# Sample rows of the mixer's output normed, turned and routed one block earlier, in both layers of a decoder step

## What is computed

```python
xp = layer_norm(ALPHA * xp + hp, ln_mix_g[i], ln_mix_b[i])      # 256 prompt rows
xs = layer_norm(ALPHA * xs + hs, ln_mix_g[i], ln_mix_b[i])      # 64 sample rows
aff = sigmoid(x @ router)                  # 32 affinities per token
grp = argmax over 4 groups of the sum of the two best (aff + bias)
eidx = the two best experts in that group; wts = aff[eidx] / sum
out = sum over the two experts of wts * (silu(x @ w_gate[e]) * (x @ w_up[e])) @ w_down[e]
x = layer_norm(ALPHA * x + out, ln_ffn_g[i], ln_ffn_b[i])
```

## Time and profile before

| | us |
|---|---|
| median of 3 runs | 1170.09 |
| lowest, highest | 1162.45, 1173.85 |
| profiled execution, its time | 1163.89 |
| span of that execution (first to last instruction) | 1160.5 |
| mean granted TensorE clock | 0.970 |
| busy: PE / DVE / ACT / POOL | 1063.1 / 455.1 / 234.7 / 131.2 |

### The profile page before, as it was taken

One profiled execution on the slowest core, in us unless ns is written; L12 is line 12 of the kernel. 1 busy time (PEld: TensorE's weight loads), 2 busy tenths in 40 slices (PEclk: granted clock), 3 DMA queues, 4 the chain that ended last, 5 costly groups with the idle time before them and its releaser, 6 DMA issues. The chain is left out here.

```text
span 1160.5 us, 13972 instructions
## 1 busy us (share of the span) xinstructions
PE 1063.1 (92%) x4918; PEld 544.3 (47%) x4918; DVE 455.1 (39%) x1167; ACT 234.7 (20%) x552; POOL 131.2 (11%) x197
## 2 busy tenths in 40 slices
PE   8899999998999989998888799899899899998883
PEld 6577767674334543333333466455554433333321
DVE  0788655546655552211111833222114522211117
ACT  0211223115001311111111313322113121111112
POOL 0000104100000011111110022320000111111010
PEclk9899999999999999999998799999999999999997
DMA  7129511205354989999998765563258599999993
GB/s 283 66 107 363 210 73 45 108 30 223 145 225 156 414 348 425 425 420 425 423 422 352 278 221 174 171 220 125 110 235 336 176 419 425 420 424 421 421 370 117
DMA packets 54913, 312.01 MB, mean 269 GB/s; under 512 B 13058, under 2 KB 13954, under 8 KB 34242
## 3 DMA queue, kind: packets, MB, share of 16 engines
q1 hardware_dynamic: 43426, 298.04, 64.3%
q0 software_dynamic: 11264, 12.61, 3.3%
q10 hardware_dynamic: 160, 0.52, 0.1%
HBM read 300.61 MB, written 33.59 MB: 288 GB/s over the span
## 5 line engine op out<-in xcount | busy, mean ns | idle before, releaser
L1402 PE MATMUL ps<-ring,xsT 128*64 128x512 f32 x704 | 160.9, 610 | 22.1 <-DMA ring<-in_experts 17.8
L1757 DVE TENSOR_TENSOR work<-work,ps 128x256 f32<-128x256 f32 x32 | 13.5, 421 | 268.6 <-ACT work L1486 268.6
L434 PE MATMUL ps<-XT,ring 128*128 128x320 f32 x384 | 108.1, 446 | 9.8 <-DMA ring<-in_w_in 5.3
L1402 PEld LDWEIGHTS ps<-ring,xsT 128*64 128x64 f32 x704 | 54.6, 140 | 125.4 <-issue 117.7
L434 PEld LDWEIGHTS ps<-XT,ring 128*128 128x128 f32 x384 | 75.3, 197 | 41.8 <-issue 7.5
L1402 PE MATMUL ps<-hi,xsT 128*64 128x512 f32 x320 | 75.7, 628 | 8.6 <-DMA hi<-in_experts 8.6
L1429 PE MATMUL ps<-ring,hT 128*64 128x512 f32 x352 | 80.4, 598 | 1.5 <-ACT hT L1490 0.9
L366 PE MATMUL ps<-XT,ring 128*128 128x320 f32 x256 | 76.9, 445 | 0.0
L1551 POOL DMA_INDIRECT y_dram<-ys,index x32 | 32.4, 1012 | 376.3 <-DVE ys L1789 333.7
L1327 PE MATMUL ps<-C 128*128 128x512 f32 x140 | 71.6, 631 | 0.6 <-PEq L836 0.3
L1543 POOL DMA_INDIRECT XT<-x_dram,index x32 | 32.8, 1024 | 314.0 <-DVE index L1686 282.3
(11 more groups left out here) (358 smaller groups left out, 1390.4 us busy)
## 6 DMA issues: line engine op xcount, KB each, us to landing
ring<-in_experts SPq DMA_DIRECT2D x36, 2048.0 KB, 24.5
ring<-in_experts SPq DMA_DIRECT2D x60, 1024.0 KB, 22.2
hi<-in_experts SPq DMA_DIRECT2D x20, 2048.0 KB, 24.6
hi<-in_experts SPq DMA_DIRECT2D x20, 1024.0 KB, 27.5
ring<-in_w_in SPq DMA_DIRECT2D x9, 2048.0 KB, 12.4
ring<-in_latent SPq DMA_DIRECT2D x60, 256.0 KB, 4.3
ring<-in_w_out SPq DMA_DIRECT2D x4, 2048.0 KB, 7.4
ring<-in_state SPq DMA_DIRECT2D x4, 1024.0 KB, 7.8
```

The lines of the kernel that those rows point to most:

```text
L434: return pe.matmul(ps[:, q, 0:TOK], ring[:, u, k * 512 + q * P:k * 512 + (q + 1) * P], XT[:, k, :], start=(k == 0), stop=(k == KD - 1))
L1402: mm = pe.matmul(ps[e * SLOTS:(e + 1) * SLOTS, GU[p], :].rearrange("p (g f) -> p g f", g=2), xsT[:, p, k, e * SLOTS:(e + 1) * SLOTS], w[:, ...
```

## The change

The class `PromptNorm` becomes `RowNorm`: every operation takes `ROWS[t]` rows, and the sample tile t = 2 goes through it at the end of the block ahead. `add_rows(v, 2)` waits for `split_done`. TensorE does three fill matmuls, then the sample tile's transposes and router matmuls (`sample_logits`); its PSUM banks are `2 * (t % 2)` and the next. ScalarE does `sample_rows`, the sigmoid's table load among it. The store of the sample rows moves from ScalarE's queue to SyncE's, behind the loads of the block's last expert. The expert block loses these operations, and six calls of idle work with them; its ScalarE begins with the sigmoids. The memset of `aff` covers 64 rows of one tile instead of all.

In the window, `turn_weights` moves behind `gate_up(0)`, ScalarE's copy of them behind `rows_in(0)`, VectorE's `weigh` behind `rows_in(0)`, and the idle call ahead of `gate_up(1)` is left out. The sample tile no longer counts in `order`, the index by which later norm steps wait.

In the diff, `expert_layer`'s lists stand behind those of the block ahead (shown for layer 0; `attend` has the same lines, the store behind `first_expert(sp, 1, 2)`).

```diff
+        FILL = 3
-        class PromptNorm:
+        class RowNorm:
...
             def turn_rows(self, pe, t):
+                r, bank = ROWS[t], 2 * (t % 2)
                 pe.wait_ge(self.norm_set, t + 1)
                 for half in range(2):
                     for k in range(4):
                         at = (4 * half + k) * P
-                        tr = pe.transpose(ps[:, 2 * t + half, k * P:(k + 1) * P], X[:, t, at:at + P], ident)
+                        tr = pe.transpose(ps[:, bank + half, k * P:k * P + r], X[0:r, t, at:at + P], ident[0:r, 0:r])
                     tr.then_inc(self.x_turned, 1)
+
+            def sample_logits(self, pe):
+                for _ in range(FILL):
+                    pe.matmul(ps[:, self.GB, :], ident, C[:, 0:512], start=True, stop=True)
+                self.turn_rows(pe, 2)
+                self.logits(pe, 2)
...
             def add_rows(self, v, t):
...
-                v.wait_ge(self.rows_done, t + 1)
+                if t == 2:
+                    v.wait_ge(self.split_done, 1)
+                else:
+                    v.wait_ge(self.rows_done, t + 1)
...
+            def sample_rows(self, act):
+                self.statistics(act, 2)
+                act.activation(self.junk[:, 0:1], eps[:, 0:1], ACT.Sigmoid)
+                self.flipped_act(act, 2)
...
                      sp.wait_ge(wout_used, 4)
                     first_expert(sp, 0, 3)
+                    norm.store(sp, 2)
...
 +                    norm.sample_logits(pe)
...
 +                    norm.sample_rows(act)
...
 +                    norm.add_rows(v, 2)
+                    norm.scale_rows(v, 2)
+                    norm.flipped_dve(v, 2)
...
 -                    idle_work(5, 6)
-                    turn_rows(pe, 0, 2)
-                    idle_work(1, 6)
-                    pe.wait_ge(xt_act, 1)
-                    pe.wait_ge(xt_dve, 1)
-                    router_logits(pe, 2).then_inc(logit_done, 1)
-
                     idle_work(8, 6)
...
                         idle_work(4, 6)
-                        turn_weights()
                         turn(w, 0)
                         gate_up(0)
+                        turn_weights()
                         turn(w, 1)
                         for j in range(PAIRS):
                             if j + 1 < LAST:
-                                idle_work(1, MAP)
+                                if j:
+                                    idle_work(1, MAP)
                                 gate_up(j + 1)
...
 -                    statistics(act, 0, 2, 0)
-                    act.activation(spare[:, 0:1], eps[:, 0:1], ACT.Sigmoid)
-                    act.wait_ge(norm_set, 1)
-                    act.dma_start(x_dram[SAMPLE, :], X[0:ROWS[2], 2, :]).then_inc(x_out, 16)
-                    flipped_act(act, 0, 2)
-                    act.wait_ge(logit_done, 1)
...
+                        rows_in(0)
                         act.wait_ge(comb_turned, 1)
                         act.activation(comb[:, :], ps[:, MAP, 0:TOK], ACT.Copy).then_inc(comb_in, 1)
-                        rows_in(0)
...
 ...
-                    step.mark(v.memset(aff[:, :, :], 0.5))
+                    step.mark(v.memset(aff[64:P, 2, :], 0.5))
...
+                        rows_in(0)
                         weigh(each)
-                        rows_in(0)
```

More of the change, by code:

```diff
@@ L259, in norm_columns, with __init__ @@
             return tr
-        class PromptNorm:
+        class RowNorm:
             GB = 6
-            def __init__(self, s, layer, junk):
+            def __init__(self, s, layer, junk, split_done=None):
                 (self.rows_done, self.summed, self.mean_set, self.squared, self.std_set, self.inverted, self.norm_set,
@@ L270, in __init__ @@
                      "n_gb_made", "n_gb_set", "n_x_turned", "n_xt_act", "n_xt_dve"])
-                self.layer, self.junk = layer, junk
+                self.layer, self.junk, self.split_done = layer, junk, split_done
             def turn_columns(self, pe):
@@ L312, in flipped_dve @@
                 for k in range(4, KD):
-                    ins = v.tensor_scalar(XT[:, k, OFF[t]:OFF[t] + P], ps[:, 2 * t + 1, (k - 4) * P:(k - 3) * P],
+                    ins = v.tensor_scalar(XT[:, k, OFF[t]:OFF[t] + ROWS[t]],
+                                          ps[:, 2 * (t % 2) + 1, (k - 4) * P:(k - 4) * P + ROWS[t]],
                                           gb[:, 0, 0, k:k + 1], gb[:, 0, 1, k:k + 1], ALU.mult, ALU.add)
@@ L839, in states_and_output @@
                 Cm = buf(st, "Cm", [P, GROUPS, 2, 4 * 40])
-                norm = PromptNorm(s, 0, Cm[:, :, :, :].rearrange("p g u x -> p (g u x)")[:, 0:D])
+                norm = RowNorm(s, 0, Cm[:, :, :, :].rearrange("p g u x -> p (g u x)")[:, 0:D])
                 pmask = buf(st, "pmask", [64, 4])
@@ L856, in states_and_output @@
                      "rstds_done", "scaled_s", "wout_used", "out_done", "state_out", "split_done", "z_ready", "gated"])
+                norm.split_done = split_done
                 block = st.enter_context(nc.Block())
@@ L1009, in _ @@
                             norm.logits(pe, blk - 14)
+                    norm.sample_logits(pe)
                 @block.scalar
@@ L1044, in _ @@
                     act.activation(ps[0:64, SB + 1, :], ps[64:P, SB, :], ACT.Copy).then_inc(split_done, 1)
+                    norm.sample_rows(act)
                 @block.vector
@@ L1126, in _ @@
                         norm.flipped_dve(v, t)
+                    norm.add_rows(v, 2)
+                    norm.scale_rows(v, 2)
+                    norm.flipped_dve(v, 2)
         def expert_layer(layer, afterwards):
@@ L1198, in order @@
                 def order(part, t):
-                    return 1 + t if part else t - 2
+                    return t
                 def load_windows(eng):
@@ L1595, in flat2 @@
                         return x.rearrange("p k t -> p (k t)")
-                    xt = X[0:64, 2, :]
-                    step.mark(v.scalar_tensor_tensor(out=xt, in0=xt, scalar=ALPHA, in1=before(2), op0=ALU.mult,
-                                                     op1=ALU.add, accum_out=row_sum[0:64, 0, 2:3]))
-                    mean(v, step, 2)
-                    step.mark(v.memset(aff[:, :, :], 0.5))
-                    scale_rows(v, step, 0, 2)
-                    v.tensor_scalar(xt, xt, mean_neg[0:64, 0, 2:3], rstd_row[0:64, 0, 2:3],
-                                    ALU.add, ALU.mult).then_inc(norm_set, 1)
-                    flipped_dve(v, 0, 2)
+                    step.mark(v.memset(aff[64:P, 2, :], 0.5))
+                    step.settle(v)
+                    v.sem_inc(mean_set, NT)
                     v.wait_ge(aff_done, 1)
@@ L2242, in attend @@
                 v_done, v_copied, wo_used, split_done = s("v_done"), s("v_copied"), s("wo_used"), s("split_done")
-                norm = PromptNorm(s, 1, pTp[:, :, :].rearrange("p u k -> p (u k)"))
+                norm = RowNorm(s, 1, pTp[:, :, :].rearrange("p u k -> p (u k)"), split_done)
                 block = st.enter_context(nc.Block())
@@ L2496, in _ @@
                             prompt_normalise(2 * n + 3)
-                    for t in range(2):
+                    for t in range(NT):
                         norm.add_rows(v, t)
```

27 lines of the change are left out of this document (14 added, 13 removed).

## The result

The changed kernel takes 1173.68 us (median of 20 runs, 1168.77 to 1180.53), the kernel before 1168.9 (20 runs, 1162.45 to 1174.11): ratio 1.0055, 95% interval 1.0038 to 1.0073. The medians are 4.8 us apart, and the interval of the ratio means 4.4 to 8.5 us slower. My sum had 0.9 slower, which I called no change. So a small slowdown, clear of the noise, came where I forecast none; the time itself lies in the stated range. The profiled execution took 1169.52, its span is 1167.8.

What follows compares the result with a forecast made beforehand. Prediction: the stream of expert weights bounds each expert layer, from its restart on. Layer 1 gains 2.8, layer 0 loses 3.7: +0.9 on a mean of 1167.6 gives 1168.5 us, called no change; range 1159 to 1177.

Steps and rivals of the forecast that it cites:

- The store: Layer 0: on SyncE's queue the store lands with expert 3's load at 413.2; gather and stream restart come 3.7 later.
- Covered, so nothing: Layer 0: a half-clock first gate-up behind the late gather is hidden by expert 5's load until about 427; costs nothing.
- Rival C: Layer 0: TensorE's clock falls in its new wait, stays down beyond the first gate-up; 3 to 8 more, 1172 to 1177; chance 0.12.
- The index and the first gather follow rigidly: Layer 1: the 1.55 gained at the sigmoids by the earlier norm passes whole to the index and first gather.
- The window: Layer 1: weights turned later, so the gather's landing decides the turn; 1.25 gained, the later `gate_up(1)` hidden.
- rival D: Layer 1: the cover of `gate_up(1)` is thinner than 2.1, 1.3 is given back; +2.2, 1169.8; chance 0.08.
- A: Layer 0: the store isn't held up, the index's 1.6 is gained; together -4.4 or -6.2, 1162 to 1163; chance 0.15.
- B: Layer 1: the clock stays up in the fill; -4.6 + 3.7, 1166.7; chance 0.2.
- Rival L: Ahead of the expert layers: something common to kernels with the new class costs 3 us; from the experiments, no chance given.

Runs made afterwards that it cites:

- e1: The changed kernel with the sample rows' store put back on ScalarE's queue; ratio to the kernel before 0.9974.
- e2: The kernel before with one part alone: SyncE instead of ScalarE issues the sample rows' store, ahead of expert 5's load; ratio 1.0019.
- e7: The changed kernel, store still on SyncE's queue but in layer 0 issued ahead of expert 3's loads; ratio to the kernel before 0.9996.
- e12: e1 unchanged, run again on one chip with the changed kernel; 1165.9 us, ratio to the kernel before 0.9999.
- e8: The changed kernel with nine instead of four idle calls ahead of layer 0's first turn; ratio to the kernel before 1.0019.
- e11: The changed kernel, unchanged, profiled a second time; no time or ratio is given.
- e6: e1 with one fill call put back between the sample tile's transposes and router matmuls; not quicker than e1, no figure given.
- e9: e6 with six instead of four idle calls ahead of layer 0's first turn; ratio to the kernel before 1.0006.
- e3: The kernel before with the window's part of the change alone; ratio 0.9986 or 0.9984 (text leaves open which), not told from the kernel before.
- e4: e1 with the window's part undone, so the norm's part alone; ratio 0.9986 or 0.9984 (text leaves open which), not told from the kernel before.
- e10: The kernel before, unchanged, profiled a second time; no time or ratio is given.
- e13: The changed kernel, unchanged, timed on one chip beside e12 and profiled a third time; 1171.96 us, ratio to the kernel before 1.0044.
- e5: e1 with six instead of eight idle calls ahead of the position sums; not quicker than e1, no figure given.

## Why the prediction was wrong

**The sum and its parts.** I had -2.8 for layer 1 and +3.7 for layer 0. The terms below measured -1.0 at layer 1's restart and +4.2 at layer 0's, and behind layer 0's restart came 2.0 more that I had put at nothing. The base moved too: the kernel before has a median of 1168.9 where I had taken 1167.6.

**The store.** Right, nearly to the digit: it was to land at 413.2, 27.3 behind the copy, and landed 27.3 behind. The term was 3.7 and measured 4.2 (32.79, the mean of three profiles, less 28.55, the mean of two): GpSimd's first gather started 0.9 behind the landing (417.02 to 416.1), not the 0.3 that I took from its wait for the index. e1, e2, e7 and e12 show that the store's place in the queue is the cause.

**"Covered, so nothing", layer 0.** This step failed, and with the next one it turned no change into slower. The halves' issue did come before expert 5's load had landed, but each request came 2 to 2.6 later relative to the stream, the cover was worked out for the first one only, and the stream lost 0.7 MB in its first 30 us: 1.7, 1.6 and 2.6 us in three profiles (231.60, 231.46, 232.44 against 229.86). e8 takes it back, so it is the clock. Rival C (0.12) had the place and kind right, but not the course: only the first gate-up was slow, and the second ended 2.6 late, inside the 4 that C calls its cover. It cost 2.0 where C has 3 to 8, so that C's 1172 to 1177 holds the result is luck: the 1.8 that layer 1 failed to gain fills the rest.

**"The index and the first gather follow rigidly", layer 1.** It failed too. The sigmoids came 1.85 earlier (1.55 forecast), and the fill ran at half clock as taken (4.52; 4.3 forecast). But I had left out the eight idle calls. They start with the sigmoids and stand ahead of the position sums, so their length is on the path, and in two of three profiles they met a half clock (in the first, granted 0.50 over 898.7 to 900.7). They took 8.65, 9.87 and 7.11; VectorE waited 1.1 for the sums in the first and not at all before. In e11 the first gate-up was slow as well (8.78). The restart moved by -1.8, +1.5 and -2.8, on average -1.0, where I forecast -2.8; only the third execution is as forecast. e6 and e9 show that the dropped call takes part in it, but with the call back the restart came no earlier (35.7), and why the clock falls in one execution and not in another stays open.

**The window.** 1.25 forecast for the turn, 1.0 found there and at the restart in e3 against e2. But the later `gate_up(1)` wasn't hidden, as I had it: the stream behind the restart loses about 0.6 with the window's order. So rival D (0.08), which has 1.3, came true in part. In layer 0 the window was worth nothing or up to 0.5.

**Sum by measured terms:** 4.2 + 2.0 in layer 0, -1.0 at layer 1's restart and 0.3 in the stream behind it: +5.5, against 4.8 between the medians and 0.38 to 0.73% (4.4 to 8.5 us). Between layer 0's combining matmuls and layer 1's split copy the changed kernel's profiles show 235.6, 236.0 and 235.2, the two of before 234.8: another 0.8 whose cause I haven't tested. It is small beside what this stretch does elsewhere (233.9 in e8, 238.6 in e12), one reason why the landmarks of single executions don't add up to the difference of the medians.

**The rivals.** A is refuted by the store's landing, B by the 4.4 to 4.5 of the fill in three profiles; e4 and e12, with the same norm, did run that fill at full clock (2.82). Rival L is neither shown nor excluded: the time ahead of layer 0's copy is 385.7 to 398.5 in the four profiles of kernels that are the same there (before, e10, e2, e3), and 388.8 to 394.4 in the eleven others. What e12 against e13 shows doesn't depend on it.

**Two readings.** The page's chain has DMA as its largest single line (8%), but TensorE's lines together are 12%; that the stream of weights sets the pace rests on the stretches, not on the chain. And rival A's best case is 1167.6 - 6.2 = 1161.4, not 1162.

## What to carry to other kernels

When a small store moves to another queue, count what stands ahead of it there: here it landed after 22.6 us instead of 7.5, and placing it one load earlier was as good as the other queue. A new wait of an engine can have a second price behind it, its clock, and a cover has to be checked for every later request of the stream, not for the first alone. Filler calls become part of the critical path once the work that they bridged gets shorter. And a gain at a landmark is worth what is left of it at the layer's end: the window's 1.0 and the earlier gathers of e5 and e6 were spent again behind it.

## What the runs showed that I had not expected

- The DMA share was 1.01 at 398 GB/s and 1.03 at 435 (from 20 to 30 us behind the restart): the share alone nearly hid the loss.
- TensorE's clock, at 1.00 while it worked up to 415.1, was 0.50 at 418 to 420 with no work at all, and 0.62 at 426 to 428, two to four us into the first gate-up.
- The clock's course differs between kernels with the same instructions in the stretch (6.23 against 4.5 for layer 1's fill), and repeated between two executions of the kernel before (e10). In the changed kernel (three courses of layer 1) and in e1's (two) it did not.
- A gather that waits for a landing started 0.9 to 1.0 behind it (changed kernel, e2, e8), one that waits for VectorE's index 0.3 behind.
